# S5 recurrence on VectorE alone, convolution taps and mean sums in another order

## The reference

```python
# S5: 64 groups of 16 channels, 64 complex states each
bu = einsum('gnp,blgp->blgn', b_bar, uf)
states[t] = lam_bar * states[t-1] + bu[t]        # complex, over the sequence
y = einsum('gpn,blgn->blgp', c_mat, states).real + d * uf
ya = gelu(y); ya = ya * sigmoid(ya @ w_glu + b_glu); ya = ya * silu(a_z)
# convolution: 31 taps, causal, per channel
h = b_val * sigmoid(b_gate)
h = conv31(h) + b_dw
h = silu(layer_norm(h))                          # mean and variance over 1024 channels
yb = (h @ w_pw + b_pw) * silu(b_z)
x = x + rms_norm(concat(ya, yb) @ ev_w_out)
```

## Time and profile before

| | |
|---|---|
| median of 3 runs | 1866.54 us (1865.88 to 1867.85) |
| span of the profiled execution | 1866.3 us |
| TensorE busy | 1687.3 us, 90% of the span |
| VectorE busy | 1004.8 us, 54% |
| ScalarE busy | 610.0 us, 33% |
| GpSimd busy | 300.8 us, 16% |
| mean granted TensorE clock | 0.964 |

### The profile page before, as it was taken

One profiled execution on the slowest core, in us unless ns is written; L12 is line 12 of the kernel. 1 busy time (PEld: TensorE's weight loads), 2 busy tenths in 40 slices (PEclk: granted clock), 3 DMA queues, 4 the chain that ended last, 5 costly groups with the idle time before them and its releaser, 6 DMA issues.

```text
span 1866.3 us, 20364 instructions
## 1 busy us (share of the span) xinstructions
PE 1687.3 (90%) x7867; PEld 1370.3 (73%) x7867; DVE 1004.8 (54%) x1271; ACT 610.0 (33%) x844; POOL 300.8 (16%) x322
## 2 busy tenths in 40 slices
PE   1699998999999999989987795889989999999995
PEld 0577887887888888878975575767877778787774
DVE  1227435455235434552999989984473344454445
ACT  2323332223221214252330222545254335243341
POOL 2297000000000000021069647300000000000000
PEclk9899999999999999999998897999989999999998
DMA  7454633333333332235321132124321323132211
GB/s 118 134 138 124 158 103 109 94 102 113 102 101 94 98 101 92 90 120 195 91 81 56 57 101 88 49 68 148 113 59 56 91 68 102 56 95 63 68 46 57
DMA packets 141323, 177.15 MB, mean 95 GB/s; under 512 B 62603, under 2 KB 73275, under 8 KB 140219
## 3 DMA queue, kind: packets, MB, share of 16 engines
q1 hardware_dynamic: 127003, 173.36, 30.4%
q10 hardware_dynamic: 13824, 2.15, 0.9%
q0 software_dynamic: 416, 0.54, 0.3%
HBM read 161.34 MB, written 14.68 MB: 94 GB/s over the span
## 4 chain that ended last, share of the span: by engine, by line
PE 73%; DVE 18%; DMA 2%; ACT 2%; issue 2%; ACTq 2%; POOL 1%; POOLq 0%; DVEq 0%
PE PS L1953 64%; DVE TMP L1632 7%; DMA LS<-in_s_log_dt_dram 2%; DVE WL L1288 2%; PE PS L1931 1%; PE PS L2195 1%; PE PS L2213 1%; DVE FIX L1669 1%; ACTq L884 1%; DVE S L1671 1%; PE PS L2204 1%; PE PS L2064 1%; PE PS L1984 1%; ACT XN L899 1%; DVE V L1366 1%
## 5 line engine op out<-in xcount | busy, mean ns | idle before, releaser
L1953 PE MATMUL PS<-HH,WH 128*128 128x512 f32 x1216 | 484.8, 399 | 46.7 <-DVE WL L1288 38.6
L1288 DVE TENSOR_TENSOR WL<-WR,WH 128x1024 fp32r<-128x1024 f32 x200 | 250.7, 1263 | 465.9 <-ACT WH L894 465.7
L1953 PE MATMUL PS<-HL,WH 128*128 128x512 f32 x1216 | 479.8, 395 | 0.0
L1953 PE MATMUL PS<-HH,WL 128*128 128x512 f32 x1216 | 479.5, 394 | 0.0
L894 ACT ACTIVATE WH<-WR 128x1024 fp32r<-128x1024 f32 x200 | 210.4, 1058 | 705.8 <-PE PS L1953 694.6
L1953 PEld LDWEIGHTS PS<-HH,WH 128*128 128x128 f32 x1216 | 232.6, 191 | 102.7 <-DVE WL L1288 26.9
L1953 PEld LDWEIGHTS PS<-HL,WH 128*128 128x128 f32 x1216 | 232.7, 191 | 48.9 <-issue 1.0
L1953 PEld LDWEIGHTS PS<-HH,WL 128*128 128x128 f32 x1216 | 232.2, 191 | 49.5
L1632 DVE SCALAR_TENSOR_TENSOR TMP<-CP,PRM,TMP 128x512 f32<-128x512 f32 x232 | 184.8, 847 | 0.0
L1953 PE MATMUL PS<-WH,HH 128*128 128x512 f32 x384 | 152.9, 398 | 15.8 <-DVE WL L1288 14.2
L1953 PE MATMUL PS<-WH,HL 128*128 128x512 f32 x384 | 151.7, 395 | 0.0
(11 more groups left out here) (309 smaller groups left out, 2063.9 us busy)
## 6 DMA issues: line engine op xcount, KB each, us to landing
WR<-in_w_in_dram SPq DMA_DIRECT2D x96, 512.0 KB, 3.8
WR<-in_ev_w_in_dram SPq DMA_DIRECT2D x40, 512.0 KB, 3.7
WR<-in_od_w_in_dram SPq DMA_DIRECT2D x32, 512.0 KB, 3.9
WR<-in_ev_w_out_dram SPq DMA_DIRECT2D x16, 512.0 KB, 3.9
WR<-in_od_w_in_dram SPq DMA_DIRECT2D x32, 256.0 KB, 3.4
WR<-in_od_w_out_dram SPq DMA_DIRECT2D x16, 512.0 KB, 3.9
WR<-in_w_branch_a_dram SPq DMA_DIRECT2D x8, 512.0 KB, 3.8
WR<-in_w_branch_b_dram SPq DMA_DIRECT2D x8, 512.0 KB, 3.7
```

Source lines behind the costliest of these rows:

```text
L1288: dve.tensor_tensor(WL[:, s, :, :], WR[:, s, :, :], WH[:, s, :, :].bitcast(F32), ALU.subtract).then_inc(w_lo, 1)
L1953: mm = pe.matmul(out_banks[m], st, mv, start=(kt == 0 and i == 0), stop=(kt == 2 * per - 1 and i == 2))
```

## The change

The recurrence runs on VectorE alone, for all 32 pairs, in operations four times as wide as VectorE's before; so do the carries and the corrections. GpSimd keeps the table of powers and signals it (`powers`). No tap runs among the recurrence's operations: `split_recur` paces them between the weight splits by a nominal cost in microseconds. Of the taps, 92 stand before the recurrence as before; 24 after it, 8 in the YL loop, 24 with the splits of glu.1 as before; the rest stands later than before: 16 with the splits of ev_a.0 (after the products of glu.0), 20 with those of ev_a.1, 64 after them. The corrections alternate two FIX buffers. The job mean stands between ev_a.0 and ev_a.1 instead of in front of ev_a.0, var behind ev_a.1. On ScalarE the emptying of ev_a.0 stands ahead of the squares and that of ev_a.1 ahead of the root.

```diff
-        SEG1 = put("SEG1", "R5", [2, PAIRS, SEG])
-        SEG2 = put("SEG2", "R5", [2, PAIRS, SEG], skip=2048)
-        SEGV = put("SEGV", "R5", [2, 2, PAIRS - PP, SEG], skip=4096)
+        SEGV = put("SEGV", "R5", [2, 2, PAIRS, SEG])
...
@@ GpSimd
-            with pool.Fori(0, SEG_CH - 1) as j:
...
-            for g in range(1, SEG):
...
-            for n, (b, ri) in enumerate(FIX_POOL):
...
+            pool.tensor_scalar(LAM64[:, 2, :].unsqueeze(2), TAB[:, 1, :, SEG_CH - 1:SEG_CH], -1.0, None,
+                               ALU.mult, ALU.bypass).then_inc(powers, 1)
@@ ScalarE
+            split()
+            act.wait_ge(h_lo, 32)
+            evac("ev_a.0", [YO[:, m, 0:NC] for m in range(4)], ACT.Copy)
             for kt in range(KT):
                 act.wait_ge(z_cent, kt + 1)
                 act.activation(SQ[:, kt, :], CP[:, kt, CPAD:], ACT.Square).then_inc(z_sq, 1)
             split()
-            act.wait_ge(h_lo, 32)
-            evac("ev_a.0", [YO[:, m, 0:NC] for m in range(4)], ACT.Copy)
+            evac("ev_a.1", [YO[:, m, NC:D] for m in range(4)], ACT.Copy)
             act.wait_ge(sq_used, KT)
...
-            split()
-            evac("ev_a.1", [YO[:, m, NC:D] for m in range(4)], ACT.Copy)
@@ VectorE
-            def step_ops():
+            def recurrence():
-                sv = S[:, :, PP:PAIRS, :].rearrange("p r g (s j) -> p r g s j", j=SEG_CH)
+                sv = S[:, :, :, :].rearrange("p r g (s j) -> p r g s j", j=SEG_CH)
                 w1, w2 = SEGV[:, 0], SEGV[:, 1]
-                shape = [P, 2, PAIRS - PP, SEG]
+                shape = [P, 2, PAIRS, SEG]
...
+                    first = seq.inc(dve.tensor_tensor(w1, LAM[:, 0:1, :].unsqueeze(3).to_broadcast(shape), now, ALU.mult))
+                    yield 0.69
+                    second = seq.inc(dve.tensor_tensor(w2, LAM[:, 1:3, :].unsqueeze(3).to_broadcast(shape), now, ALU.mult))
+                    yield 0.69
+                    seq.wait(first)
+                    third = seq.inc(dve.tensor_tensor(nxt, nxt, w1, ALU.add))
+                    yield 0.69
+                    seq.wait(third)
+                    seq.inc(dve.tensor_tensor(nxt[:, 1:2], nxt[:, 1:2], w2[:, 0:1], ALU.add))
+                    yield 0.43
+                    last = seq.inc(dve.tensor_tensor(nxt[:, 0:1], nxt[:, 0:1], w2[:, 1:2], ALU.add))
+                    yield 0.43
+                dve.wait_ge(powers, 1)
...
+                used = [last, last]
+                for b in range(FIX_BLOCKS):
+                    for q in range(2):
+                        made = []
+                        for ri in range(2):
+                            fix, into, by, end, op = correction(b, ri, q, ri)
+                            seq.wait(used[ri])
+                            made.append(seq.inc(dve.tensor_tensor(fix, by, end, ALU.mult)))
+                            yield 0.59
+                        for ri in range(2):
+                            fix, into, by, end, op = correction(b, ri, q, ri)
+                            seq.wait(made[ri])
+                            used[ri] = seq.inc(dve.tensor_tensor(into, into, fix, op))
+                            yield 0.59
...
+            def split_recur(states, us):
+                for q in range(4):
+                    spent = 0.0
+                    while spent < us:
+                        spent += next(states, us)
+                    split(1)
             split_convolve(24)
             split_convolve(24)
             convolve(44)
-            steps = step_ops()
-            split_convolve(20, steps)
-            split_convolve(12, steps)
+            s5 = recurrence()
+            split_recur(s5, 4.2)
+            split_recur(s5, 4.2)
             times_tmp([("b_gate.1", m, CP[:, 4 + m, CPAD:]) for m in range(4)], GATEV)
             dve.wait_ge(tmp_free, 24)
-            split_convolve(20, steps)
-            split_convolve(24, steps)
-            for _ in steps:
+            split_recur(s5, 3.6)
+            split_recur(s5, 4.2)
+            split_recur(s5, 4.2)
+            for _ in s5:
                 pass
-            split_convolve(8)
-            dve.wait_ge(carried, 1)
...
             split()
             convolve(24)
...
             split_convolve(24)
-            convolve(len(todo))
             for u in range(2):
                 if u:
-                    split()
+                    split_convolve(16)
                     h_low(3, lambda kt: YA[:, kt, :], range(4))
                 dve.wait_ge(ya_gated, 4 * u + 4)
                 times_tmp([(f"glu.{u}", m, YA[:, 4 * u + m, :]) for m in range(4)], GLUV)
             h_low(3, lambda kt: YA[:, kt, :], range(4, 8))
+            split_convolve(20)
+            convolve(len(todo))
@@ TensorE
-                pe.wait_ge(fixed_pool, i + 1)
-                pe.wait_ge(fixed_dve, i + 1)
+                pe.wait_ge(fixed, i + 1)
...
+            section("ev_a", H, ready(h_lo, 3), rows=True, units=(0,))
             pe.wait_ge(ones_in, 1)
             pe.wait_ge(conv_done, 8)
             free("mean")
...
-            section("ev_a", H, ready(h_lo, 3), rows=True, units=(0,))
+            section("ev_a", H, ready(h_lo, 3), rows=True, units=(1,))
             free("var")
...
-            section("ev_a", H, ready(h_lo, 3), rows=True, units=(1,))
             section("pw", Y, ready(y_lo, 4))
```

More of the change, by code:

```diff
@@ L40 @@
 FB = 4
-FIX_POOL = [(b, 0) for b in range(7)]
-FIX_DVE = [(b, 1) for b in range(8)] + [(7, 0)]
-FIX_HALF = 4
 PAIRS = D // (2 * S5_GROUP)
-PP = PAIRS - 8
+FIX_BLOCKS = PAIRS // FB
 HEADS = 4
@@ L128 @@
 _section("glu", a=4)
+_add("ev_a.0", 4, 0, 4)
 _add("mean", side=1, d=1)
-_add("ev_a.0", 4, 0, 4)
+_add("ev_a.1", 4, 0, 4)
 _add("var", a=1)
-_add("ev_a.1", 4, 0, 4)
 _section("pw", d=4)
@@ L821, in _ @@
-            seq.base, seq.n = 0, first + per_step * (SEG_CH - 1)
-            pool.wait_ge(states, SEG_CH)
-            pool.wait_ge(dve_states, 1)
-            for g in range(1, SEG):
[L826 to L836, removed]
@@ L837, in _ @@
-            pool.wait_ge(carried, 1)
-            for n, (b, ri) in enumerate(FIX_POOL):
[L840 to L849, removed]
+            pool.tensor_scalar(LAM64[:, 2, :].unsqueeze(2), TAB[:, 1, :, SEG_CH - 1:SEG_CH], -1.0, None,
+                               ALU.mult, ALU.bypass).then_inc(powers, 1)
@@ L1621, in convolve @@
-            def convolve(n, steps=None):
+                    yield 0.43
+                    last = seq.inc(dve.tensor_tensor(nxt[:, 0:1], nxt[:, 0:1], w2[:, 1:2], ALU.add))
+                    yield 0.43
+                dve.wait_ge(powers, 1)
+                s1, s2 = ST1[:, :, :].unsqueeze(3), ST2[:, :, :].unsqueeze(3)
+                for g in range(1, SEG):
+                    now, nxt = [S[:, :, :, SEG_CH * k - 1:SEG_CH * k] for k in (g, g + 1)]
+                    seq.wait(last)
+                    first = seq.inc(dve.tensor_tensor(s1, LAM64[:, 0:1, :].to_broadcast([P, 2, PAIRS]).unsqueeze(3), now, ALU.mult))
+                    yield 0.23
+                    second = seq.inc(dve.tensor_tensor(s2, LAM64[:, 1:3, :].unsqueeze(3), now, ALU.mult))
+                    yield 0.23
+                    seq.wait(first)
+                    third = seq.inc(dve.tensor_tensor(nxt, nxt, s1, ALU.add))
+                    yield 0.23
+                    seq.wait(third)
+                    seq.inc(dve.tensor_tensor(nxt[:, 1:2], nxt[:, 1:2], s2[:, 0:1], ALU.add))
+                    yield 0.2
+                    last = seq.inc(dve.tensor_tensor(nxt[:, 0:1], nxt[:, 0:1], s2[:, 1:2], ALU.add))
+                    yield 0.2
@@ new lines, in recurrence @@
+                seq.wait(last)
+                dve.memset(BNA[:, 0, 0:1], 0.0).then_inc(carried, 1)
+                used = [last, last]
[12 more added lines that the diff above has]
+                            yield 0.59
+                    if b % 4 == 3:
+                        seq.wait(used[1])
+                        dve.memset(BNA[:, 0, 0:1], 0.0).then_inc(fixed, 1)
@@ L1638, in convolve, with split_convolve @@
                     conv["i"] += 1
[L1639 to L1640 removed]
             dve.wait_ge(tmp_free, 20)
             dve.wait_ge(m_acc, 16)
[L1644 removed]
+            def split_convolve(n):
                 for q in range(4):
[L1647 removed]
+                    convolve(n // 4)
+                    split(1)
[4 more added lines that the diff above has]
+                        spent += next(states, us)
                     split(1)
```

36 lines of the change are left out of this document (2 added, 34 removed).

## The result

The kernel after the change takes 1893.06 us (median of 4 runs, 1891.14 to 1894.48) against 1867.19 us for the kernel before in the same session: ratio 1.0136, 95% interval 1.0121 to 1.015. That is 1.4% slower. The forecast was 0.2% slower; 1893 lies above the top of its range, 1878. The profiled execution spans 1889.4 us, 23.1 more than before, where the working had 4.1.

A forecast was written before the change was run, and what follows sets the result against it. VectorE, slowed beside GpSimd, was taken to bound the recurrence. b_z2.1 ends 35.7 us earlier, but late taps and an open chain after var start pw.0 4.1 us later: 1870.7 us, range 1855 to 1878.

The forecast's parts named there:

- What bounds the kernel before: In the recurrence stretch, VectorE, slowed while GpSimd runs its part, is what everybody waits for; 51 us lost.
- Step 1, the recurrence: Recurrence on VectorE alone: 101 us of operations, eight quarters of 7.2 us against TensorE's 5.44; b_z2.1 ends 35.7 us earlier.
- E: End of b_z2.1, the last unit of the recurrence stretch: forecast 1091.6 us, before 1127.3; break-even 1087.5.
- the clock loss of 1.9 us: After a 3.5 us stall ahead of a_z2.1, TensorE runs at a lowered clock for a while, losing 1.9 us.
- the two bounds: Price of a strided 512-element VectorE operation: 0.60 us as side by side, or 0.94 at 1.7 ns per element; 0.93 taken.
- Rival A: Recurrence: strided 512-wide operations run as side by side, VectorE never late, b_z2.1 ends 1076.1; total 1855.1 us; chance 0.19.
- Rival B: Within 0.2%: mechanism as forecast, but strided 512 at 0.85 us or YL loop 4 us less; 1864 to 1869; chance 0.12.
- Rival C: Recurrence: TensorE's clock drops at each stall in the eight late quarters, 8 us at most; 1874 to 1879; chance 0.11.
- Steps 2 and 3: From b_z2.1's end to the mean: 30.2 us to first YA, VectorE idle 12; then 125.7 us, 64 taps lying bare.
- Step 4, after the mean: Mean to pw.0: 49.3 us, including an open 9.7 us chain after var; DMA loads as before; pw.0 starts 4.1 us later.
- M: Start of the mean's matmuls, forecast at 1247.5 us, 155.9 us after the end of b_z2.1.
- The direction: Chances for the whole kernel: slower 0.45, same 0.30, faster 0.25.

The follow-up runs named there:

- experiment 6: Kernel before with GpSimd's 15 recurrence steps left out (24 of 32 pairs not advanced), VectorE's work unchanged: 1813.0 us, ratio 0.9701.
- experiment 1: Kernel after with SP issuing pw's loads ahead of its wait for var's squares and of the X1 load: 1876.13 us, ratio 1.0039 to the kernel before.
- experiment 4: Kernel after with the recurrence steps addressing 8 neighbouring elements instead of every 16th, same operation count and sizes: 1876.0 us, ratio 1.0041 to the kernel before.
- Experiment 5: Kernel after with finer pacing, one recurrence step of five operations between two weight splits, stride unchanged: 1875.28 us, ratio 1.0038 to the kernel before.
- Experiment 2: Kernel before with only mean and var moved (engine orders to match), recurrence and taps as before: 1903.82 us, ratio 1.0184.
- experiment 3: Kernel after with mean and var moved back and the last 84 taps in one piece ahead of the mean: 1876.61 us, ratio 1.0047 to the kernel before.
- Experiment 7: experiment 1's kernel with both ev_a units ahead of mean and var, pw.0's splits among the last taps, 24 taps brought forward: 1841.99 us, ratio 0.9852.

## Why the prediction was wrong, step by step

**What bounds the kernel before**: right. VectorE set the pace through GpSimd's share of the recurrence; without GpSimd's steps b_z2.1 ends 50.0 us earlier (experiment 6), and the working had found 51 lost up to there.

**Step 1, the recurrence**: right in the mechanism and in the sum, and the exactness is luck. E, the end of b_z2.1, was forecast at 1091.6; ScalarE's row at 1092.66 stands 35.7 us before that of the earlier trace rows, the very gain forecast. The operation was taken at 0.93 us and cost 0.97; a quarter with its split came to 7.4 us against 7.2, 1.5 us more in eight. Against that the recurrence began 1.2 us earlier (956.47 against 957.7), and the clock loss of 1.9 us did not come in this execution: the stall ahead of a_z2.1 showed 1.8 us where 3.5 was forecast, and the granted clock from 1022 to 1030 us was 1.00. It did come in the profiled execution of experiment 1, whose program is the same up to there: a stall of 3.4 us, a granted clock of 0.60 from 1022 to 1030 us, and b_z2.1 emptied 1.4 us later, at 1094.04. The line through the sizes 64 and 128 held up to 512, and of the two bounds it was the upper one that counted. Rival A fell by its own sign (operations of 0.69 us), and experiment 4 shows that it had the condition and the price right: 16.4 us at the mean against 15.6. The formula that the Trainium skill gives (VectorE: DVE Perf Modes, the TRN2 errata), 0.69 us at 512 elements, holds where the elements are neighbours (0.68 to 0.69 in experiment 4) and fails here, with 1.04. The page has no term for a step and does not say that it holds for any; "whatever the step" was my reading. The Trainium skill's rule of 16-byte lines (SBUF — State Buffer, Door 1: The DMA port swizzle) had the direction: the trace agrees, with 0.35 us more at 512.

**Rival B** needed a strided operation of 0.85 us; it cost 0.97. **Rival C**, a clock that drops at each stall, did not come. TensorE's seven waits for WL were up to 1.8 us, and its granted clock from 957 to 1022 us was 0.97; VectorE set the pace of these quarters whatever the clock.

**Steps 2 and 3**: right. VectorE idled 11.8 us before the first YL (12 forecast), TensorE 44.5 us before the mean (44), and the mean began at 1248.0 (1247.5). Small slips in the working change nothing: 24 taps and 4 splits are 20.4 us by its own prices, not 21.0; the unit that ScalarE empties after E is b_z2.1, not b_z2.0; and B's 0.12 is split into 0.06 and 0.05. Experiment 5 confirms that the mean follows E: 14.7 us earlier there, 15.4 earlier here.

**Step 4, after the mean**: the step that failed, with the sentence "The change moves no DMA; the loads follow the splits in SP's queue as before, with four slots ahead". The first half is true and the second is not. The loads of pw do not follow the splits alone: they stand behind `sp.wait_ge(sq_used, KT)`, and that wait is released by var, which the change moved. The working had the emptying of ev_a.1 done by M + 34, under var; behind the late loads it ended at 1303.1, M + 55. Mean to var's end was forecast at 37.6 us and took 38.0; then the chain to pw.0 was forecast at 9.7 and took 28.1. The 18.4 us are the working's miss: 4.1 forecast, 18.4 here and 0.5 and 0.4 from M and the sums make 23.4, and the spans differ by 23.1. Experiment 1 takes this one wait away (and with it the place behind X1's load) and comes to 1876.13, near the forecast's 1870.7 (what is left, some 5 us, is 3.4 of a later mean and 0.6 of slower matmuls from there to var's end in that trace; the rest is not resolved). Experiment 2 shows it belongs to the move of the mean, and experiment 3 that it goes with it.

**The direction** was right, and not by the queue's wait alone: slower had the largest chance, and without that wait the kernel is still 0.4% slower (experiment 1). No rival held the queue's wait. It would have been found by asking, for var and not only for the loads, who else waits for this job: TensorE, ScalarE and VectorE were asked, SP was not.

**Where the gain went.** Taking the steps off GpSimd brings the end of b_z2.1 forward by 50.0 us (experiment 6); with VectorE doing them itself 35.7 of these arrive there, and with the finer pacing of experiment 5 all of them (50.4). From there they are lost three times: 12 us idle on VectorE before YA, 64 taps that lie bare ahead of the mean, and the wait in SP's queue. Experiment 7 gets most of all three back (1.4 us of idle time, 10.7 ahead of the mean, 9.8 ahead of pw.0) and is 51 us faster than the kernel after.

## What to carry to other kernels

When a job moves, look in every queue for waits that this job releases, the DMA queue's above all: a load that stands behind such a wait moves with the job, however many slots are free, and so does all that an engine has behind its first use of the load (here ScalarE's root). Work taken out from under a slow stretch comes due somewhere; find the next idle time of the same engine and put it there before counting a gain. And if an engine that paces another has idle time further on, make its portions fit the other's (5.25 us from split to split against 5.44 here) before making its operations faster: both gave the same 16 to 18 us here, and the finer pacing gave nothing once that idle time was filled.

## What the hardware showed unexpectedly

A VectorE operation on fp32 data in steps of 64 bytes costs 1.04 us at 512 elements against 0.69 on neighbours, 0.64 against 0.42 at 256, and 0.37 against 0.29 (worked out) at 128: the dearer the wider, so that making strided operations wide saves the fixed part only.

GpSimd beside VectorE costs more than its own work suggests. 15 steps on GpSimd cost the kernel before 54 us; and eight products moved from GpSimd to VectorE made VectorE's loop shorter by 2.8 us, since from the third YL of 128x512 on each took 1.68 to 1.79 us beside them, and 0.68 to 0.69 without.
